# A projection stage continued inside the feed-forward block before it, and transposes of the first projection alternated with its first products

## The chip, the cores and the metric

The kernel runs on one core of one Trainium2 chip. The metric is device time in microseconds (us) of one execution; the time before the change is 2881.29 us, the median of 3 runs (2877.69 to 2884.19). TensorE is PE in the rows, VectorE is DVE, ScalarE is ACT, GpSimd is POOL, and SP is SyncE's queue.

## The reference

Two transformer blocks run one after the other on x of 1024 tokens by 1024 channels, all in float32:

```python
def first_block(x, ...):
    h = rms_norm(x, mix_norm_g) @ w_in            # 1024 x 2568: q, k, v, 8 forget gates, z
    merged = concat(rms_norm(forgetting_attention(q, k, v, log_f)), rms_norm(spatial_gating(gelu(z))))
    x = x + merged @ w_out
    gate, up = split(rms_norm(x, ffn_norm_g) @ w_gate_up)     # 1024 x 2*2816
    x = x + (silu(gate) * up) @ w_down
    return rms_norm(x, final_norm_g)

def second_block(x, ...):
    proj = rms_norm(x, w_norm_mix) @ w_mix_in     # 1024 x 3592: short conv, gated delta net, stick-breaking attention
    x = x + concat(y_sc, y_gdn, y_sb) @ w_mix_out
    gate, val = split(causal_dwconv(rms_norm(x, w_norm_ffn) @ w_ffn_up, w_ffn_conv))
    x = x + (silu(gate) * val) @ w_ffn_down
    return rms_norm(x, w_norm_final)
```

## The kernel before

Every product of float32 matrices is made of three TensorE products of rounded halves: value = hi + lo, and hi x hi, hi x lo, lo x hi are summed in PSUM. The activations stand transposed in SBUF as `xt_hi` and `xt_lo` (8 slices of 128 channels, 1024 tokens). Weights come in slices of 128 x 512: SyncE loads one into one of four `w_raw` buffers, GpSimd splits it into `w_hi` and `w_lo` (lines 115 and 117, or 278 and 280, 950 and 952), TensorE uses it. Semaphores order all this: `m.loaded`, `m.split`, `m.used`; PSUM has eight banks of 128 x 512.

The program is a list of stages, each a block of five instruction lists, one for each engine; a stage starts when all engines have left the one before. The ones that matter here:

- `first_stage` (projection 1). Tokens are normed in pairs of 128-token tiles: VectorE and ScalarE each square one tile (`square`, `square_pair`), ScalarE makes the reciprocal root, VectorE scales both tiles (`scale`). TensorE transposes half the tokens of one channel slice with four 128 x 128 transposes into a bank (`turn(h, k)`, half h, slice k, line 295); ScalarE rounds the bank to `xt_hi` (`high`), VectorE writes the rest to `xt_lo` (`low`, line 438). Four banks, 4 to 7, serve the transposes in rotation, so `turn` number n waits for `low` number n-4. TensorE does all eight `turn(0, k)` first, then the first chunk of products for the first half of the tokens (lines 315 to 317, banks 0 to 3), with the `turn(1, ...)` pairs after slices 3 to 6, then the second half.
- `mlp_stage` (output projection, norm, feed-forward). It is used twice, plain and with the causal convolution (tiles with `_conv`). The hidden channels go in 11 steps of 256: `up` products, hidden values, `down` products added to `x_sb`. The last step has its own code: its `up` slices 4 to 7 go to `end_hi` and `end_lo`, its four down slices go to the ring `w_hi`, `w_lo` again, and `split_slices(m, pool, last + 12, DN)` makes GpSimd wait until the down products of the step before are through with that ring place. TensorE waits for all four (`pe.wait_ge(m.split, last + 12 + DN)`), then does the last down products tile by tile (lines 1044 to 1046, `last_hi`, `last_lo`).
- The end of the plain `mlp_stage`: for each tile t VectorE adds the two banks (`last_down`, line 1375), ScalarE squares and makes the root (`square_rstd`, line 1120), VectorE scales by the gain (`normed`, line 1381), ScalarE squares again, VectorE scales into `scaled_out` (`rescale`, line 1387), SyncE stores `x_sb` to DRAM. Then TensorE transposes all of `scaled_out` in 16 turns over eight banks (line 1102), ScalarE writes `xt_hi` (line 1208), VectorE `xt_lo` (`low`, line 1234). GpSimd splits the first four slices of the next projection once all tiles are scaled.
- `proj2_stage` (projection 2). SyncE loads 8 gate columns (`w_ab`), GpSimd splits them, TensorE multiplies them with all tokens (lines 1482 to 1484, 48 products), then does seven chunks of 512 columns with `chunk_products` (line 169), 192 products each. ScalarE empties the banks and turns the gate values; VectorE scans them; TensorE transposes them (`gate_columns`, in chunk 1); then the convolution jobs follow the chunks.

Of the kernel before, what the change touches and what calls it, by code (L numbers as in the profile page):

```python
# [5 lines left out]
ALU = mybir.AluOpType  # L6
# [6 lines left out]
P = 128  # L13
# [171 lines left out]
def first_stage(m, x_sb, zu, zv, v, q, k_, sp_f, csum, sums_dram, w_sT):  # L185
# [34 lines left out]
    with nc.Block() as block:  # L220
# [67 lines left out]
        def _(pe):  # L288
# [130 lines left out]
        def _(dve):  # L419
# [30 lines left out]
            dve.tensor_copy(m.cols[:, COL_FFC + 88:COL_FFC + 132], m.psum[0][:, 2 * P:2 * P + 44]).then_inc(cols_done, 1)  # L450
            dve.wait_ge(cols_done, 3)
# [10 lines left out]

            dve.wait_ge(vec_turned, 2)
# [389 lines left out]
def mlp_stage(m, tag, w_out, scales, load_x, gcol, w_up, w_down, x_sb, conv, gain, store, next_gcol=None, first=None):  # L853
# [17 lines left out]
    spare = [m.at(f"scaled_out{i}" + tag, [P, 4, D], (16, 152)[i]) for i in range(2)]  # L871
    junk = m.at("mlp_squares" + tag, [P, 4, D], 176)
# [12 lines left out]
    GU, DN = 8, 4  # L885

# [8 lines left out]
    with nc.Block() as block:  # L895
        @block.sync
        def _(sp):
# [26 lines left out]
            if first is not None:  # L924
                load_first(m, sp, base + 16 + 12 * FI, first)
# [3 lines left out]
            sp.wait_ge(stored, 16 * NT)  # L929

        @block.gpsimd
        def _(pool):
# [25 lines left out]
            split_slices(m, pool, last + 12, DN)  # L958
            if first is not None:
                pool.wait_ge(scl, 2 * NT)  # L960
                split_first(m, pool, base + 16 + 12 * FI)

        @block.tensor
        def _(pe):
# [76 lines left out]
            def down_bank(hi, lo, bank, t, nh, done):  # L1041
                for j in range(2):
                    u, tok = 2 * nh + j, slice(t * P, (t + 1) * P)
                    pe.matmul(m.psum[bank][:, :], hi[:, j, tok], m.w_hi[:, u, :], start=j == 0, stop=False)  # L1044
                    pe.matmul(m.psum[bank][:, :], lo[:, j, tok], m.w_hi[:, u, :], start=False, stop=False)  # L1045
                    mm = pe.matmul(m.psum[bank][:, :], hi[:, j, tok], m.w_lo[:, u, :], start=False, stop=j == 1)  # L1046
# [39 lines left out]
            for t in range(NT):  # L1086
                if t in (0, 4):
                    pe.wait_ge(hid, 4 * (FI - 1) + 2 * (t // 4) + 2)
                for nh in range(2):
                    if t >= 4:  # L1090
                        pe.wait_ge(dn_ev, 16 * (FI - 1) + NB + 2 * (t - 4) + nh + 1)
                    down_bank(last_hi, last_lo, (2 * t + nh) % NB, t, nh, dn_done)
            if next_gcol is not None:
                for n in range(2 * KD):
                    h, k = n // KD, n % KD
                    if k == 0:
                        pe.wait_ge(scl, NT + 4 * (h + 1))
                        pe.wait_ge(dn_ev, 16 * FI + NB)
                    if n >= NB:
                        pe.wait_ge(t_lo, 16 + n + 1 - NB)  # L1100
                    for j in range(4):
                        mm = pe.transpose(m.psum[n % NB][:, j * P:(j + 1) * P], spare[h][:, j, k * P:(k + 1) * P], m.ident[:, :])
                    mm.then_inc(turned, 1)
# [12 lines left out]
        counts = {"square": 0, "log": 0, "rstd": 0}  # L1116

# [12 lines left out]
        def _(act):  # L1130
# [66 lines left out]
            for t in range(NT + 1):  # L1197
                if t < NT:
                    act.wait_ge(dn_ev, 16 * (FI - 1) + NB + 2 * t + 2)
                    square_rstd(act, 1, t, junk[:, t % 2, :])  # L1200
# [1253 lines left out]
```

## Time and profile before

| what | us |
|---|---|
| median of 3 runs | 2881.29 |
| the profiled execution, its own time | 2874.96 |
| span of the profiled execution | 2872.9 |
| TensorE busy in the span | 2724.7 (95%) |
| VectorE busy | 1298.7 (45%) |
| GpSimd busy | 1175.0 (41%) |
| ScalarE busy | 665.7 (23%) |

The times of the rows below are those of the profiled execution, from the start of its span. A row of the timeline gives start, duration, engine, line, operation, output and input, count, and in brackets the idle time of the engine just before and what ended it.

### The profile page before, as it was taken

Reading aid. Unit: us, or ns where it says so; the run is one execution under the profiler, and the core shown is the slowest. Engines: PE = TensorE matmul, PEld = TensorE weight load, DVE = VectorE, ACT = ScalarE, POOL = GpSimd, SP = SyncE. Lnnn points to the kernel's source line nnn. Section 1 sums busy time; section 2 is a strip of 40 time slices with the busy share of each in tenths; the row PEclk is TensorE's granted clock in tenths of the full one; section 3 lists DMA queues with packets and bytes.
Section 4 is the critical chain, followed back from the end, with each engine's and each line's share of the span. In section 5 each row is a group of like instructions: output and inputs, shape, how many; then the busy total and the mean of one; then the engine's idle time right before and its main releaser. Section 6 shows DMA issues by size and latency. Waiting matters only on the chain. (4 is left out here: it accounts for less than half of the span.)

```text
span 2872.9 us, 34847 instructions
## 1 busy us (share of the span) xinstructions
PE 2724.7 (95%) x12979; PEld 2183.2 (76%) x12979; DVE 1298.7 (45%) x1808; ACT 665.7 (23%) x1250; POOL 1175.0 (41%) x919
## 2 busy tenths in 40 slices
PE   7999879999999999979999888879999999999998
PEld 6786447888888888857888677864688888888876
DVE  3133432334333333461451466667234555666667
ACT  2201651200000001141222233245222211111123
POOL 4441134244444444423454333340324454555552
PEclk9999999999999999989999899989999999999999
DMA  3111003111111111121111000000311111111111
GB/s 121 47 48 37 30 16 117 30 52 47 51 47 49 49 48 47 55 89 39 50 48 41 1 1 1 1 16 1 118 30 41 48 44 51 47 50 48 47 55 73
DMA packets 91017, 131.61 MB, mean 46 GB/s; under 512 B 9269, under 2 KB 57632, under 8 KB 90920
## 3 DMA queue, kind: packets, MB, share of 16 engines
q1 hardware_dynamic: 88288, 121.76, 14.0%
q10 hardware_dynamic: 2632, 8.51, 0.7%
q8 instruction: 67, 1.10, 0.2%
q14 instruction: 30, 0.25, 0.0%
HBM read 121.82 MB, written 8.42 MB: 45 GB/s over the span
## 5 line engine op out<-in xcount | busy, mean ns | idle before, releaser
L115 POOL TENSOR_TENSOR w_hi<-w_raw,zero 128x512 fp32r<-128x512 f32 x336 | 395.1, 1176 | 1063.6 <-PE bank L1012 450.5
L117 POOL TENSOR_TENSOR w_lo<-w_raw,w_hi 128x512 fp32r<-128x512 f32 x336 | 485.0, 1443 | 26.4
L1010 PE MATMUL bank<-xt_hi,w_hi 128*128 128x512 f32 x1248 | 485.7, 389 | 1.6 <-DVE x_sb L1220 0.8
L1011 PE MATMUL bank<-xt_lo,w_hi 128*128 128x512 f32 x1248 | 485.5, 389 | 0.0
L1012 PE MATMUL bank<-xt_hi,w_lo 128*128 128x512 f32 x1248 | 485.5, 389 | 0.0
L1318 DVE TENSOR_TENSOR x_sb<-bank,x_sb 128x512 f32<-128x512 f32 x320 | 221.3, 692 | 202.9 <-PE bank L1046 202.5
L1010 PEld LDWEIGHTS bank<-xt_hi,w_hi 128*128 128x128 f32 x1248 | 234.2, 188 | 51.1 <-DVE x_sb L1220 1.3
L1012 PEld LDWEIGHTS bank<-xt_hi,w_lo 128*128 128x128 f32 x1248 | 234.2, 188 | 48.7
L1011 PEld LDWEIGHTS bank<-xt_lo,w_hi 128*128 128x128 f32 x1248 | 234.2, 188 | 48.6
L169 PE MATMUL bank<-xt_hi,w_hi 128*128 128x512 f32 x512 | 199.4, 390 | 0.0
L169 PE MATMUL bank<-xt_lo,w_hi 128*128 128x512 f32 x512 | 199.2, 389 | 0.0
L169 PE MATMUL bank<-xt_hi,w_lo 128*128 128x512 f32 x512 | 199.2, 389 | 0.0
L1276 DVE COPY hidden_raw<-bank 128x512 f32<-128x512 f32 x44 | 30.5, 692 | 326.0 <-PE bank L1012 325.9
L1285 DVE SCALAR_TENSOR_TENSOR hidden_conv<-hidden_raw_conv,cols,hidden_conv 128x1024 f32<-128x1024 f32 x80 | 156.0, 1979 | 6.6 <-ACT hidden_conv L1143 1.3
L1764 POOL TENSOR_TENSOR LM<-LT,levels 128x1024 f32<-128x1024 f32 x24 | 64.1, 2677 | 155.1 <-DVE LT L1912 83.8
L1044 PE MATMUL bank<-w_hi,hidden_hi 128*128 128x512 f32 x320 | 124.5, 389 | 0.0
L1045 PE MATMUL bank<-w_hi,hidden_lo 128*128 128x512 f32 x320 | 124.5, 389 | 0.0
L1044 PE MATMUL bank<-w_hi,hidden_hi_conv 128*128 128x512 f32 x320 | 124.5, 389 | 0.0
L1045 PE MATMUL bank<-w_hi,hidden_lo_conv 128*128 128x512 f32 x320 | 124.5, 389 | 0.0
L1046 PE MATMUL bank<-w_lo,hidden_hi 128*128 128x512 f32 x320 | 124.5, 389 | 0.0
L1046 PE MATMUL bank<-w_lo,hidden_hi_conv 128*128 128x512 f32 x320 | 124.5, 389 | 0.0
L169 PEld LDWEIGHTS bank<-xt_hi,w_hi 128*128 128x128 f32 x512 | 96.1, 188 | 20.4 <-ACT ab L1523 0.4
(466 smaller groups left out, 4820.0 us busy)
## 6 DMA issues: line engine op xcount, KB each, us to landing
w_raw<-in_w_gate_up_dram SPq DMA_DIRECT2D x88, 256.0 KB, 3.1
w_raw<-in_w_ffn_up_dram SPq DMA_DIRECT2D x88, 256.0 KB, 3.1
w_raw<-in_w_mix_in_dram SPq DMA_DIRECT2D x56, 256.0 KB, 2.7
w_raw<-in_w_down_dram SPq DMA_DIRECT2D x44, 256.0 KB, 2.8
w_raw<-in_w_ffn_down_dram SPq DMA_DIRECT2D x44, 256.0 KB, 2.8
w_raw<-in_w_in_dram SPq DMA_DIRECT2D x40, 256.0 KB, 2.7
x_sb<-in_x_dram SPq DMA_DIRECT2D x4, 1024.0 KB, 8.4
gate_rows<-gate_sums SPq DMA_DIRECT2D x8, 512.0 KB, 4.6
```

Source lines behind the costliest of these rows:

```text
L115: pool.tensor_tensor(m.w_hi[:, u, :], m.w_raw[:, u, :], zeros, ALU.add).then_inc(m.hi_done, 1)
L117: pool.tensor_tensor(m.w_lo[:, u, :], m.w_raw[:, u, :], m.w_hi[:, u, :].bitcast(F32), ALU.subtract).then_inc(m.split, 1)
L169: mm = pe.matmul(m.psum[b][:, :], lhs, rhs, start=k == 0 and i == 0, stop=k == KD - 1 and i == 2)
L1010: pe.matmul(m.psum[b][:, :], u_hi[:, col], m.xt_hi[:, k, tok], start=k == 0, stop=False)
L1011: pe.matmul(m.psum[b][:, :], u_hi[:, col], m.xt_lo[:, k, tok], start=False, stop=False)
L1012: mm = pe.matmul(m.psum[b][:, :], u_lo[:, col], m.xt_hi[:, k, tok], start=False, stop=k == KD - 1)
L1044: pe.matmul(m.psum[bank][:, :], hi[:, j, tok], m.w_hi[:, u, :], start=j == 0, stop=False)
L1045: pe.matmul(m.psum[bank][:, :], lo[:, j, tok], m.w_hi[:, u, :], start=False, stop=False)
L1046: mm = pe.matmul(m.psum[bank][:, :], hi[:, j, tok], m.w_lo[:, u, :], start=False, stop=j == 1)
L1285: ins = dve.scalar_tensor_tensor(mix[:, c, :], raw[:, c, PAD - back:PAD - back + S], weights_of(i, c, 2 - back), mix[:, c, :], ALU.mult, A ...
L1318: dve.tensor_tensor(xs, m.psum[t][:, :], xs, ALU.add).then_inc(dn_ev, 1)
L1764: pool.tensor_tensor(LM[j % 2][:, :, :], LT[:, :, :], lev[:, j, :].unsqueeze(1).to_broadcast([P, NT, P]), ALU.mult).then_inc(pool_s, 1)
```

## The change

There are four parts.

1. `proj2_stage` no longer opens a block. It returns an object whose five functions are called at the end of the plain `mlp_stage`'s five lists. No engine waits there for the others.
2. The join itself. The 16 turns of `scaled_out` use banks 0 to 3 in rotation. The rounding of turns 0 and 1 is queued on ScalarE and VectorE at tile 6 of the last tile loop, that of turns 2 and 3 at tile 7, the rest behind it (`turns_at`). The first chunk of projection 2 goes by token halves: TensorE turns slices 0 to 7 of the first half, multiplies the first half into banks 4 to 7 with the turns of the second half in pairs after slices 3 to 6, then the second half into banks 3 to 0. The gate columns' products follow chunk 0 instead of preceding it, and `gate_columns` moves from chunk 1 to chunk 2. Slices 4 to 7 of chunk 0 are split into `end_hi`, `end_lo`. ScalarE waits for the stores of `x_sb` before it empties chunk 0. Two scratch tiles move.
3. In `mlp_stage`, both uses: the four down slices of the last step are split into `end_hi`, `end_lo`, as soon as the last `up` products no longer read these.
4. In `first_stage`: `turn(0, 4)` to `turn(0, 7)` go one ahead of each of the products of slices 0 to 3; the pairs of `turn(1, ...)` follow slices 4 to 7 instead of 3 to 6; the waits of the first half for `t_lo` 5 to 8 go. On VectorE the copies of the gain columns come before `scale(1)`, and the copy of the identity to bfloat16 goes behind the last `low`.

```diff
@@ first_stage, TensorE
-            for k in range(KD):
+            for k in range(4):
                 turn(0, k)
             pe.wait_ge(cols_done, 3)
             for h in range(2):
                 for k in range(KD):
+                    if h == 0 and k < 4:
+                        turn(0, 4 + k)
...
                     for b in range(4 * h, 4 * h + 4):
-                        if k == 0:
-                            pe.wait_ge(t_lo, 5 + b if h == 0 else 9 + b)
+                        if h and k == 0:
+                            pe.wait_ge(t_lo, 9 + b)
...
-                    if h == 0 and 3 <= k < 7:
-                        turn(1, 2 * (k - 3))
-                        turn(1, 2 * (k - 3) + 1)
+                    if h == 0 and k >= 4:
+                        turn(1, 2 * (k - 4))
+                        turn(1, 2 * (k - 4) + 1)
@@ first_stage, VectorE
-            for j in range(2):
-                square(j)
-                scale(j)
-            dve.wait_ge(masked, 1)
-            dve.tensor_copy(m.ident_b[:, :], m.ident[:, :])
+            square(0)
+            scale(0)
+            square(1)
             dve.wait_ge(made, 5)
             dve.wait_ge(vec_turned, 1)
...
+            scale(1)
             dve.wait_ge(cols_done, 3)
...
+            dve.wait_ge(masked, 1)
+            dve.tensor_copy(m.ident_b[:, :], m.ident[:, :])
@@ mlp_stage, GpSimd
-            split_slices(m, pool, last + 12, DN)
-            if first is not None:
-                pool.wait_ge(scl, 2 * NT)
-                split_first(m, pool, base + 16 + 12 * FI)
+            for u in range(DN):
+                n = last + 12 + u
+                pool.wait_ge(m.used, last + RING + u + 1)
+                pool.wait_ge(m.loaded[u], 16 * (n // RING) + 16)
+                pool.tensor_tensor(end_hi[:, u, :], m.w_raw[:, u, :], zeros, ALU.add).then_inc(m.hi_done, 1)
...
+            if nxt is not None:
+                nxt.gpsimd(pool)
@@ mlp_stage, TensorE
+            def turn_next(h, k):
+                n = KD * h + k
+                pe.wait_ge(scl, NT + 4 * (h + 1))
+                if n < 4:
+                    pe.wait_ge(dn_ev, 16 * (FI - 1) + NB + 8 + n + 1)
+                else:
+                    pe.wait_ge(t_lo, 16 + n - 3)
+                for j in range(4):
+                    mm = pe.transpose(m.psum[n % 4][:, j * P:(j + 1) * P], spare[h][:, j, k * P:(k + 1) * P], m.ident[:, :])
+                mm.then_inc(turned, 1)
+
+            if nxt is not None:
+                for k in range(KD):
+                    turn_next(0, k)
+                nxt.tensor(pe, turn_next, t_lo, dn_ev)
@@ mlp_stage, ScalarE and VectorE
+        turns_at = {NT - 2: (0, 1), NT - 1: (2, 3), NT: tuple(range(4, 2 * KD))}
...
+            if nxt is not None:
+                act.wait_ge(stored, 16 * NT)
+                nxt.scalar(act)
@@ proj2_stage, GpSimd
+        for u in range(RING):
+            n = base + u
+            pool.wait_ge(m.used, n + 1 - 2 * RING)
+            split_slice(m, pool, n, n // RING, u, True)
+        for u in range(RING):
+            n = base + RING + u
+            pool.wait_ge(m.used, n + 1 - 2 * RING)
...
@@ proj2_stage, TensorE
+        for h in range(2):
+            for k in range(KD):
...
+                pe.wait_ge(m.split, base + k + 1)
+                pe.wait_ge(t_lo, 16 + 8 * h + k + 1)
+                for n in range(4):
+                    bank, col = m.psum[4 + n - 4 * h], slice(n * P, (n + 1) * P)
+                    if k == 0 and h == 0:
+                        pe.wait_ge(dn_ev, nxt.dn + 4 + n + 1)
+                    if k == 0 and h:
+                        pe.wait_ge(t_lo, 16 + 13 + n)
...
+                if h == 0 and 3 <= k < 7:
+                    turn(1, 2 * (k - 3))
+                    turn(1, 2 * (k - 3) + 1)
```

## Rows read from the trace of the kernel before

**Rows 1.** The page, part 1: busy time, share of the span, instructions.
```profile
PE 2724.7 (95%) x12979; PEld 2183.2 (76%) x12979; DVE 1298.7 (45%) x1808; ACT 665.7 (23%) x1250; POOL 1175.0 (41%) x919
```

**Rows 2.** Waits of PE: engine, line, releaser: total us, times, longest.
```profile
PE bank L1044 <- POOL w_lo L117: 8.3, 2, 4.2
```

**Rows 3.** Timeline of the first projection's start, several engines.
```profile
15.38 6.12 PE L295 MATMUL bank<-ident,x_scaled 128*128 128x128 f32 x32 [3.52 <-DVE x_scaled L432]
...
17.81 2.76 DVE L438 SCALAR_TENSOR_TENSOR xt_lo<-bank,cols,xt_hi 128x512 fp32r<-128x512 f32 x4 [0.83 <-ACT xt_hi L377]
...
19.07 1.06 PE L295 MATMUL bank<-ident,x_scaled 128*128 128x128 f32 x4
...
26.17 0.77 PE L315 MATMUL bank<-w_hi,xt_hi 128*128 128x512 f32 x1 [4.67 <-DVE xt_lo L438]
...
27.92 1.79 DVE L427 CUSTOM_DVE_ANT_0 junk_d<-x_sb 128x1024 f32<-128x1024 f32 x1
...
30.36 2.48 DVE L432 TENSOR_SCALAR x_scaled<-x_sb,x_rstd 128x1024 f32<-128x1024 f32 x2 [0.65 <-ACT x_rstd L372]
...
32.37 1.62 POOL L280 TENSOR_TENSOR first_lo<-w_raw,first_hi 128x512 fp32r<-128x512 f32 x1
...
39.24 1.03 PE L295 MATMUL bank<-ident,x_scaled 128*128 128x128 f32 x8
...
53.75 0.39 PE L315 MATMUL bank<-w_hi,xt_hi 128*128 128x512 f32 x1
```

**Rows 4.** Windows: stretch, us, busy by engine (instructions), PEclk, DMA, GB/s.
```profile
26.00:30.50 4.50, 4.33 (x10) 3.47 (x11) 3.85 (x7) 0.71 (x4) 4.34 (x4) 0.50 0.00 0
...
1267.00:1268.00 1.00, 1.00 (x6) 1.00 (x6) 0.44 (x1) 0.97 (x3) 0.00 (x0) 0.50 0.99 406
...
1269.00:1270.00 1.00, 1.00 (x8) 0.97 (x6) 0.75 (x1) 1.00 (x3) 0.00 (x0) 0.68 0.32 131
...
1298.60:1342.40 43.80, 43.80 (x193) 35.96 (x192) 10.85 (x9) 9.05 (x13) 18.18 (x14) 1.00 0.16 43
```

**Rows 5.** Timeline, plain feed-forward's end and projection 2's start, several engines.
```profile
1234.33 0.69 DVE L1318 TENSOR_TENSOR x_sb<-bank,x_sb 128x512 f32<-128x512 f32 x1 [0.67 <-PE bank L1046]
...
1237.15 1.26 POOL L117 TENSOR_TENSOR w_lo<-w_raw,w_hi 128x512 fp32r<-128x512 f32 x1
...
1238.47 0.50 PE L1044 MATMUL bank<-w_hi,last_hi 128*128 128x512 f32 x1 [4.17 <-POOL w_lo L117]
...
1242.45 0.39 PE L1045 MATMUL bank<-w_hi,last_lo 128*128 128x512 f32 x1
...
1264.23 1.04 ACT L1120 ACTIVATE mlp_squares<-x_sb 128x1024 f32<-128x1024 f32 x1
...
1264.85 5.35 PE L1102 MATMUL bank<-ident,scaled_out 128*128 128x128 f32 x32 [2.72 <-DVE x_sb L1375]
...
1270.63 9.34 ACT L1208 ACTIVATE xt_hi<-bank,cols 128x512 fp32r<-128x512 f32 x16
...
1271.43 10.62 DVE L1234 SCALAR_TENSOR_TENSOR xt_lo<-bank,cols,xt_hi 128x512 fp32r<-128x512 f32 x16
...
1285.32 0.59 PE L1482 MATMUL bank<-xt_hi,w_ab_hi 128*8 128x512 f32 x1 [7.49 <-POOL w_ab_lo L1473]
...
1342.43 0.39 PE L169 MATMUL bank<-xt_hi,w_hi 128*128 128x512 f32 x1
```

**Rows 6.** Timeline, the last step of the feed-forward with convolution.
```profile
2796.70 11.64 DVE L1336 SCALAR_TENSOR_TENSOR hidden_conv<-hidden_raw_conv,cols,hidden_conv 128x512 f32<-128x512 f32 x8 [0.85 <-ACT hidden_conv L1161]
...
2817.92 0.74 DVE L1336 SCALAR_TENSOR_TENSOR hidden_conv<-hidden_raw_conv,cols,hidden_conv 128x512 f32<-128x512 f32 x1
...
2837.71 0.69 DVE L1318 TENSOR_TENSOR x_sb<-bank,x_sb 128x512 f32<-128x512 f32 x1 [0.67 <-PE bank L1046]
...
2841.84 0.79 PE L1044 MATMUL bank<-w_hi,last_hi_conv 128*128 128x512 f32 x1 [4.17 <-POOL w_lo L117]
...
2846.66 0.39 PE L1046 MATMUL bank<-w_lo,last_hi_conv 128*128 128x512 f32 x1
```

More of the change, by code:

```diff
@@ L1395, in _ @@
                     rescale(t - 2)
+                for n in turns_at.get(t, ()) if nxt is not None and t < NT - 1 else ():
+                    low(16 + n, n % 4, next_gcol)
             normed(NT - 1)
[L1397 removed]
+            if nxt is not None:
                 rescale(NT - 2)
+                for n in turns_at[NT - 1]:
+                    low(16 + n, n % 4, next_gcol)
                 rescale(NT - 1)
[L1400 to L1403 removed]
+                for n in turns_at[NT]:
+                    low(16 + n, n % 4, next_gcol)
+                nxt.vector(dve)
     m.slices += 16 + 12 * FI
     m.chunks += FI
+    if nxt is not None:
+        m.slices += nxt.slices
+        m.chunks += nxt.chunks
 HG = 4
 def proj2_stage(m, sc, qkv, gz, sqk, sv, gates):
[L1415 to L1416 removed]
+    a, nxt = m.a, Machine()
     w = a["w_mix_in_2"][0]
[L1418 to L1419 removed]
+    wf = m.at("w_ab", [P, KD, 8], 196.125)
+    wf_hi, wf_lo = m.at("w_ab_hi", [P, KD, 8], 196.375, F32R), m.at("w_ab_lo", [P, KD, 8], 196.625, F32R)
     conv = m.at("conv", [P, 2, S], 184)
@@ new lines, in tensor, with gate_columns, wait_bank @@
+    def tensor(pe, turn, t_lo, dn_ev):
+        base, c0 = nxt.base, nxt.c0
+        for h in range(2):
+            tok = slice(h * HALF, (h + 1) * HALF)
+            for k in range(KD):
+                if k < RING:
+                    hi, lo = m.w_hi[:, k, :], m.w_lo[:, k, :]
+                else:
+                    hi, lo = nxt.hi[:, k - RING, :], nxt.lo[:, k - RING, :]
+                pe.wait_ge(m.split, base + k + 1)
[6 more added lines that the diff above has]
+                        pe.wait_ge(t_lo, 16 + 13 + n)
+                    pe.matmul(bank[:, :], hi[:, col], m.xt_hi[:, k, tok], start=k == 0, stop=False)
+                    pe.matmul(bank[:, :], hi[:, col], m.xt_lo[:, k, tok], start=False, stop=False)
+                    mm = pe.matmul(bank[:, :], lo[:, col], m.xt_hi[:, k, tok], start=False, stop=k == KD - 1)
+                    if h and n == 3:
+                        mm.then_inc(m.used, 1)
+                    elif k == KD - 1:
+                        mm.then_inc(m.bank_done, 1)
+                if h == 0 and 3 <= k < 7:
+                    turn(1, 2 * (k - 3))
+                    turn(1, 2 * (k - 3) + 1)
+        pe.wait_ge(f_split, 2)
+        for h in range(2):
+            tok = slice(h * HALF, (h + 1) * HALF)
+            pe.wait_ge(evac, h + 1)
+            for k in range(KD):
+                pe.matmul(m.psum[4 + h][0:8, :], wf_hi[:, k, :], m.xt_hi[:, k, tok], start=k == 0, stop=False)
+                pe.matmul(m.psum[4 + h][0:8, :], wf_hi[:, k, :], m.xt_lo[:, k, tok], start=False, stop=False)
+                mm = pe.matmul(m.psum[4 + h][0:8, :], wf_lo[:, k, :], m.xt_hi[:, k, tok], start=False, stop=k == KD - 1)
+            mm.then_inc(f_done, 1)
+        def gate_columns():
+            pe.wait_ge(rows, 3)
+            pe.wait_ge(evac, 2 * NB)
+            for j in range(NT):
+                pe.transpose(m.psum[NB - 1][:, 8 * j:8 * j + 8], gc[:, j * P:(j + 1) * P], m.ident[0:8, 0:8])
+            for j in range(NT):
+                mm = pe.transpose(m.psum[NB - 1][:, 64 + 8 * j:72 + 8 * j], ab[:, j * P:(j + 1) * P], m.ident[0:8, 0:8])
+            mm.then_inc(turned, 1)
+        for c in range(1, NC):
+            def wait_bank(b):
+                if c == 1 and b in (4, 5):
+                    pe.wait_ge(f_evac, b - 3)
+                elif c == 1:
+                    pe.wait_ge(evac, (b + 4) % NB + 1)
+                else:
+                    pe.wait_ge(evac, 8 * (c - 1) + b + 1)
+                if c == 2 and b == 3:
+                    gate_columns()
+                if c == 2 and b == NB - 1:
+                    pe.wait_ge(turned, 2)
+            chunk_products(m, pe, base + 8 * c, c0 + c, c == 5, wait_bank)
```

361 lines of the change are left out of this document (169 added, 192 removed).

## The prediction

> **What bounds the kernel.** I read the page's busy shares first: TensorE is busy 95% of the span, no other engine half of it [rows 1]. So what can be won without fewer products is TensorE's idle time and the time it spends at a lower clock. The view of TensorE's waits names the places. One entry is touched by part 3 of the change: twice TensorE waits some 4 us for GpSimd's last split [rows 2]. The timelines around the edits then show each idle stretch with its releaser: 4.67 us at 26 us [rows 3]; 4.17, 2.72 and 7.49 us around 1238 to 1285 us (and a further 2.12 between the two halves of the transposes there) [rows 5]; 4.17 us again at 2842 us [rows 6]. These come to 25 us, 0.9% of the span. Last the windows: each longer stop is followed by a spell in which the granted clock is 0.50, the 1.2 GHz level: 10 products in 4.33 us at 26 us [rows 4], 0.43 us each, against 43.80 us for 193 at 2.4 GHz, 0.227 each [rows 4]. A product in such a spell costs 0.20 us more.
>
> **Part 4, the first projection.** Before, TensorE does 32 transposes from 15.38 on, then stands until 26.17, because the products' start asks for the `low` of slices 4 to 7, which stand in VectorE's list behind `square(2)` and `scale(2)`; its second half starts at 53.75 [rows 3]. After, `turn(0,4)` starts at 19.07 as before (the sixteenth transpose's end sets it, and the first `low` is done at 18.5) [rows 3]. At the clock of then, the turn ends near 19.8. From there to the second half stand 96 products (21.8 us), `turn(0,5)` to `(0,7)` and eight turns of the second half. A turn costs 0.456: between products, eight transposes push TensorE back by 0.91 (the row at 39.24 shows them [rows 3]; four pairs and their products fill 39.24 to 53.75 in this measure). That is 19.8 + 21.8 + 11 x 0.456 = 46.6. The weights don't hold it: the last split is through at 33.99 [rows 3], and it is wanted near 43.
>
> One new wait. `turn(0,7)` now ends near 29.4, so `low(0,7)` ends near 31.1, and `square(3)` and `scale(3)` stand behind it in VectorE's list. Before, `square(3)` started at 27.92 and `scale(3)` ended at 32.84, 4.9 later [rows 3]. Counted from 31.1 this is 36.0; GpSimd's last weight split ends at 33.99, after which I take the scaling somewhat faster, 35.6. `turn(1,0)` is wanted at 34.9: a stall of 0.7 (bounds 0 and 1.5). The second half starts at 47.3 instead of 53.75: **6.4 us** (5 to 7). The column copies moved ahead of `scale(1)` fit in the time in which VectorE waits for ScalarE's root. The identity copy costs nothing where it goes: VectorE is idle for the second half's products, and its reader is in the next stage.
>
> The trace also bears on whether transposes hold the clock up. In the stretch from 1264.85 TensorE does transposes alone; the clock is 0.50 at 1267 and has risen within 1269 to 1270 (0.68 over that us) [rows 4, 5]. So transposes alone let it rise, and I let the products at 19.8 start at 2.4 GHz, with no spell such as that of 26 to 30.5. The Trainium skill says the opposite in "TensorE: Matmul & The Clock Gate", section "Part 4: PE-mode transpose": transposes don't count as busy time for the clock. By it the products would begin at the lower level and the sum be as in rival A below.
>
> **Part 3, the last down slices.** TensorE starts the last down products at 1238.47, released by GpSimd. What is needed besides is VectorE's read of the bank at 1234.33 + 0.69 = 1235.02 [rows 5]. GpSimd can now split in the time in which it was idle since the last `up` products; so TensorE starts at 1235.1, 3.4 us earlier. The stop shrinks to 0.8 us and I take it to be without a spell at half clock (if not, the 3.4 alone stay); there were 3.98 us from 1238.47 to 1242.45 for 10 products worth 2.27, 1.7 more [rows 5]. The chain behind moves by **5.1 us**. In the convolution's copy the reads end at 2837.71 + 0.69 = 2838.4, the products start at 2841.84 [rows 6]: 3.4; the first 11 take 4.82 instead of 2.50: 2.3; together 5.7. Everything behind this to the end of the span is paced by these products, so it counts in full. Against it: GpSimd's four splits now fall on VectorE's tap steps. Such a step takes 0.74 alone, and 11.64/8 = 1.46 where GpSimd works beside it [rows 6]; four to five steps would lag by 3 us, and the last reads, without steps between, win most of it back. I charge 0.5 (0 to 2). **5.2 us** (3.4 to 5.7).
>
> **Parts 1 and 2, the join.** What sets its pace is ScalarE's chain of 16 square-and-root groups, 1.60 us each (four of them from 1264.23 to 1270.63) [rows 5]. The fifteenth ends at 1269.03. It comes 5.1 earlier by part 3: 1263.9. Into the chain come the `xt_hi` of turns 0 and 1, 9.34/16 = 0.58 each: 1.2. Then the square of tile 7 waits for VectorE's list, which has the two `low` (10.62/16 = 0.66 each) ahead of the two reads of tile 7: 0.8 for the second `low` and 1.3 for the reads, 2.1. So the fifteenth group ends at 1267.2. Turns 2 and 3 are rounded behind it: 1.2 on ScalarE, then 0.8 for the last `low`: 1269.2. Only then is the bank of `turn(0,7)` free; the turn costs 0.9 at half clock. First product at **1270.1**. Queued behind the same `low`s are `rescale` of tiles 6 and 7, wanted only by the second half's turns at 1283; behind the new wait for the stores stands the emptying of chunk 0's banks, first needed by the gate products at 1320, when the stores are long out.
>
> Before, with all 16 turns done, TensorE began projection 2 at 1285.32 and chunk 1 at 1342.43 [rows 5]: 57.1 us for gate products and chunk 0, with a half-clock spell at its head. After, the same products start 15.2 earlier, again after a stop and so with the same spell, and the eight turns of the second half lie between them, 3.65. That is 11.6 earlier. Removed in this are the wait for all rounding, the block's end, and the trip for `w_ab`, whose load, split and products are now covered by chunk 0. Chunk 0's slices are split in time: slices 0 to 3 while the last down products run, 4 to 7 at about 1255 to 1266, first wanted at 1283. But then GpSimd works beside VectorE's scaling. What `L1336` shows doubles an instruction [rows 6]; up to three of them lie on the path, 0 to 3 us; most fall in the 3 us in which VectorE waits for turn 0's rounding, so 0.5. **11.1 us** (7 to 13). `gate_columns` in chunk 2 waits for nothing new, since the scan is done by 1350; ScalarE's first convolution job waits some 2 us longer, under a chunk of 43.8 us.
>
> **Sum.** 6.4 + 11.1 + 5.2 = 22.7 us. The profiled execution's own time is 2874.96 (span 2872.9 and 2.1 around it), which gives 2852.3; the median of the runs is 6.3 higher, 2881.29, and the prediction for it is **2858.6**. A difference of under 0.2%, 5.8 us, can't be told from none here.
>
> **Rivals.** A: transposes don't keep the clock up. Then the first projection's products start at half clock, ten of them at 0.20 more, 2.0 to 2.2 lost: 2860.8. Against it stands the rise within 1269 to 1270 [rows 4].
> B: VectorE's order sets the join. The `low`s put ahead of tile 7 and GpSimd's splits stretch the tile loop by 5 more than I count, and the 0.7 stall becomes 1.5: gain 17, 2864.5. For it: VectorE is nearly full in the tile loop, and doubled instructions are in the trace [rows 6].
> C: part 3 does not do what it says: the last down products wait for something else that comes at the same time (the hidden values, or a late load), so 5.1 and 5.2 go; gain 12.4, 2868.9. Against it: VectorE's reads before them end on TensorE's beat in both copies [rows 5, 6].
> D, on the other side: the lower clock persists in the join. TensorE comes in with 7.5 us of idle time cut up by single turns, and if it then ran chunk 0 at 1.2 GHz throughout, 192 products would cost 38.4 us instead of the 2.2 of one spell: 36.2 - 22.7 = 13.5 us slower, 2894.8. It decides from some 125 products at half clock. Against it: every spell in the rows ends within 5 us of work [rows 4 to 6].
>
> **Chances.** Forecast 0.74, A 0.10, B 0.09, C 0.05, D 0.02. The first three reach from 2852 (all upper bounds, 7 + 13 + 5.7 = 25.7, and half of the runs' scatter) to about 2865; with C at the edge the range is 2851 to 2869. Faster by over 0.2%: 0.96, same 0.02, slower 0.02.
>
> **What would show it.** The first product of the first projection near 20 with granted clock 1.00, its second half at 47 to 48, an idle time near 0.7 before `turn(1,0)`. The last down products following the reads by 0.1, with products of 0.39 only, in both copies. Projection 2's first product near 1264 in the new count (1270.1 less the 6.4 won before), chunk 1 starting 17.5 earlier than 1342.43, no wait for the gate columns. The prediction is wrong if TensorE shows a new wait above 2 us in one of these places, or if chunk 0 runs at 0.50 for more than 5 us.

## The result and the profile after

| | kernel before | kernel after |
|---|---|---|
| median, us (runs) | 2879.49 (4: 2875.12 to 2884.19) | 2849.26 (4: 2848.04 to 2851.25) |
| profiled execution's own time | 2874.96 | 2850.17 |
| its span | 2872.9 | 2848.3 |

The ratio is 0.9895, 95% interval 0.9877 to 0.9913: the change makes the kernel 1.0% faster, 30 us in these medians. The forecast was 2858.6 with a range from 2851 to 2869: the right side, but 9.3 us too slow and outside the range. Two more sets of runs of the same program gave 2852.22 (ratio 0.9909) and 2849.26 (0.9904). One of these three medians, 2852.22, would lie inside the range. All 12 runs of the changed kernel have the median 2850.35 and the mean 2850.4; 67 runs of the kernel before have 2878.0 and 2878.6. (One further execution of the kernel before, at 4605 us with the clock at 0.555, is left out everywhere.) So the gain in means is 28.2 us, and 22.7 were forecast.

The page's part 1 of the kernel after, as [rows 1] of before: TensorE has the same 12979 products and transposes in 11.8 us less busy time. So nearly half of what the span lost, 24.6 us, is not idle time but the same work done in less time; 1.7 us of the 11.8 lie in the three unedited stages shown below. Stretches that TensorE spends at 1.2 GHz instead of 2.4 are called half clock from here on.

```profile
PE 2712.9 (95%) x12979; PEld 2175.6 (76%) x12979; DVE 1300.9 (46%) x1808; ACT 669.8 (24%) x1252; POOL 1180.3 (41%) x919
```

TensorE's waits in the kernel after. The 8.3 us for GpSimd's last split [rows 2] are gone; in their place stand 1.7 us, twice 0.8, that no releaser explains. The join now waits twice for `low`, 9.4 us in all; before, its three stops were 2.72, 2.12 and 7.49 us:

```profile
PE bank L1115 <- DVE xt_lo L1255: 9.4, 2, 5.8
...
PE bank L1058 <- issue: 1.7, 2, 0.8
```

The timeline of the first projection after, against [rows 3]. Twenty transposes, then products at once; VectorE's `scale(3)`; the last pair of turns of the second half; the first product of the second half:

```profile
16.31 4.47 PE L295 MATMUL bank<-ident,x_scaled 128*128 128x128 f32 x20 [3.15 <-DVE x_scaled L434]
20.49 0.52 PE L317 MATMUL bank<-w_hi,xt_hi 128*128 128x512 f32 x1
20.85 0.39 PE L318 MATMUL bank<-w_lo,xt_hi 128*128 128x512 f32 x1
...
33.71 1.42 DVE L434 TENSOR_SCALAR x_scaled<-x_sb,x_rstd 128x1024 f32<-128x1024 f32 x2 [0.65 <-ACT x_rstd L374]
...
46.60 1.03 PE L295 MATMUL bank<-ident,x_scaled 128*128 128x128 f32 x8
47.39 0.48 PE L317 MATMUL bank<-w_hi,xt_hi 128*128 128x512 f32 x1
```

The second half starts at 47.39 instead of 53.75. No stop stands ahead of `turn(1,0)`, which starts at 35.69: `scale(3)` ends at 35.13.

The timeline at the plain block's end and the join, against [rows 5]. Two GpSimd splits and VectorE's two scalings of the last tile, with GpSimd idle, are among the rows:

```profile
1231.11 0.69 DVE L1339 TENSOR_TENSOR x_sb<-bank,x_sb 128x512 f32<-128x512 f32 x1 [0.67 <-PE bank L1060]
1231.90 0.47 PE L1058 MATMUL bank<-end_hi,last_hi 128*128 128x512 f32 x1 [0.83 <-issue]
1232.21 0.39 PE L1059 MATMUL bank<-end_hi,last_lo 128*128 128x512 f32 x1
...
1253.22 2.25 DVE L1402 SCALAR_TENSOR_TENSOR x_sb<-x_sb,mlp_rstd,gain 128x1024 f32<-128x1024 f32 x1
...
1254.35 2.02 POOL L1520 TENSOR_TENSOR end_hi<-w_raw,zero 128x512 fp32r<-128x512 f32 x1
...
1255.39 1.53 DVE L1408 TENSOR_SCALAR scaled_out<-x_sb,mlp_rstd 128x1024 f32<-128x1024 f32 x1
...
1259.24 1.74 PE L1115 MATMUL bank<-ident,scaled_out 128*128 128x128 f32 x8 [3.54 <-DVE xt_lo L1255]
...
1260.98 1.06 ACT L1139 ACTIVATE mlp_squares<-x_sb 128x1024 f32<-128x1024 f32 x1 [2.10 <-DVE x_sb L1396]
...
1261.47 2.13 POOL L1522 TENSOR_TENSOR end_lo<-w_raw,end_hi 128x512 fp32r<-128x512 f32 x1
...
1262.39 1.75 DVE L1408 TENSOR_SCALAR scaled_out<-x_sb,mlp_rstd 128x1024 f32<-128x1024 f32 x1
...
1264.07 1.27 DVE L1402 SCALAR_TENSOR_TENSOR x_sb<-x_sb,mlp_rstd,gain 128x1024 f32<-128x1024 f32 x1
...
1265.27 0.74 DVE L1408 TENSOR_SCALAR scaled_out<-x_sb,mlp_rstd 128x1024 f32<-128x1024 f32 x1
...
1266.81 1.94 PE L1115 MATMUL bank<-ident,scaled_out 128*128 128x128 f32 x8 [5.83 <-DVE xt_lo L1255]
...
1268.40 0.78 PE L1548 MATMUL bank<-xt_hi,w_hi 128*128 128x512 f32 x1
...
1270.10 0.40 PE L1549 MATMUL bank<-xt_lo,w_hi 128*128 128x512 f32 x1
...
1327.41 0.39 PE L169 MATMUL bank<-xt_hi,w_hi 128*128 128x512 f32 x1
```

The last row is chunk 1. From the start of the last down products to it are 95.5 us; before, from 1238.47 to 1342.43, 104.0 [rows 5]. The convolution's copy now runs as the plain one:

```profile
2818.67 0.69 DVE L1339 TENSOR_TENSOR x_sb<-bank,x_sb 128x512 f32<-128x512 f32 x1 [0.67 <-PE bank L1060]
...
2819.47 0.47 PE L1058 MATMUL bank<-end_hi_conv,last_hi_conv 128*128 128x512 f32 x1 [0.83 <-issue]
```

**Where the rest is.** The edited places are covered by four stretches between fixed products of TensorE; three stretches hold code that the diff doesn't touch: attention, the gated delta net, and the stick-breaking attention with the products up to the last block's first. The windows of these three, in the profile of before and of after (columns as in [rows 4]):

```profile
266.80:438.40 171.60, 137.23 (x922) 78.77 (x921) 79.70 (x254) 97.58 (x235) 43.37 (x38) 0.94 0.08 28
1606.20:1869.50 263.30, 223.31 (x1536) 196.80 (x1536) 164.58 (x273) 85.86 (x136) 91.87 (x64) 0.91 0.00 1
1902.00:2052.40 150.40, 133.00 (x512) 70.42 (x513) 99.21 (x208) 71.37 (x157) 39.22 (x33) 0.91 0.09 33
```

```profile
260.60:435.10 174.50, 140.18 (x921) 80.61 (x921) 79.70 (x254) 97.82 (x235) 43.40 (x38) 0.92 0.08 27
1591.20:1853.00 261.80, 221.52 (x1536) 196.16 (x1536) 164.59 (x273) 85.86 (x136) 92.82 (x63) 0.92 0.00 1
1885.50:2033.30 147.80, 130.12 (x512) 68.58 (x513) 99.21 (x208) 71.30 (x157) 36.81 (x30) 0.93 0.07 26
```

The same instructions take 171.6 us in one and 174.5 in the other, 263.3 and 261.8, 150.4 and 147.8; VectorE's busy time is the same to 0.1, TensorE's is not, and the granted clock goes the other way than the length. In this pair the sum differs by only 1.2 (585.3 and 584.1). Whether it is more on average is what the later experiments ask.

### The profile page after: what moved, and what is told of

Same layout as the page of the kernel before. It is cut to its first block and busy times, and to the rows that moved or that the text cites. A ratio compares the mean times of both kernels' runs of the same rounds, so it can differ in the third digit from the quotient of the medians.

```text
span 2848.3 us, 34838 instructions
## 1 busy us (share of the span) xinstructions
PE 2712.9 (95%) x12979; PEld 2175.6 (76%) x12979; DVE 1300.9 (46%) x1808; ACT 669.8 (24%) x1252; POOL 1180.3 (41%) x919
## 5 line engine op out<-in xcount | busy, mean ns | idle before, releaser
L115 POOL TENSOR_TENSOR w_hi<-w_raw,zero 128x512 fp32r<-128x512 f32 x324 | 384.0, 1185 | 1006.7 <-PE bank L1026 450.2
L1024 PE MATMUL bank<-xt_hi,w_hi 128*128 128x512 f32 x1248 | 485.7, 389 | 1.6 <-DVE x_sb L1241 0.8
L1026 PE MATMUL bank<-xt_hi,w_lo 128*128 128x512 f32 x1248 | 485.5, 389 | 0.0
L1025 PE MATMUL bank<-xt_lo,w_hi 128*128 128x512 f32 x1248 | 485.5, 389 | 0.0
L117 POOL TENSOR_TENSOR w_lo<-w_raw,w_hi 128x512 fp32r<-128x512 f32 x324 | 468.4, 1446 | 25.3
L1024 PEld LDWEIGHTS bank<-xt_hi,w_hi 128*128 128x128 f32 x1248 | 234.2, 188 | 51.0 <-DVE x_sb L1241 1.3
L169 PE MATMUL bank<-xt_hi,w_hi 128*128 128x512 f32 x448 | 174.4, 389 | 0.0
L169 PE MATMUL bank<-xt_lo,w_hi 128*128 128x512 f32 x448 | 174.3, 389 | 0.0
L169 PE MATMUL bank<-xt_hi,w_lo 128*128 128x512 f32 x448 | 174.3, 389 | 0.0
L1154 ACT ACTIVATE hidden_raw<-bank 128x512 f32<-128x512 f32 x44 | 26.3, 601 | 360.9 <-PE bank L1026 360.8
```

Of the source, the lines that this page charges most:

```text
L115: pool.tensor_tensor(m.w_hi[:, u, :], m.w_raw[:, u, :], zeros, ALU.add).then_inc(m.hi_done, 1)
L117: pool.tensor_tensor(m.w_lo[:, u, :], m.w_raw[:, u, :], m.w_hi[:, u, :].bitcast(F32), ALU.subtract).then_inc(m.split, 1)
L169: mm = pe.matmul(m.psum[b][:, :], lhs, rhs, start=k == 0 and i == 0, stop=k == KD - 1 and i == 2)
L1024: pe.matmul(m.psum[b][:, :], u_hi[:, col], m.xt_hi[:, k, tok], start=k == 0, stop=False)
L1025: pe.matmul(m.psum[b][:, :], u_hi[:, col], m.xt_lo[:, k, tok], start=False, stop=False)
L1026: mm = pe.matmul(m.psum[b][:, :], u_lo[:, col], m.xt_hi[:, k, tok], start=False, stop=k == KD - 1)
```

## The experiments

**The theories.** They are named as in the expectations. S: each part gives its term at its own place, as the prediction says, and what the medians show beyond the sum is how the half-clock time of unedited stages happens to fall in an execution. P: the shifted start of those stages changes their half-clock time for good. B (rival B of the prediction): VectorE's order and GpSimd's splits set the join, so its part is small.

**Each part alone.** Three kernels. The first is the kernel before with part 4:

```diff
-            for k in range(KD):
+            for k in range(4):
                 turn(0, k)
...
+                    if h == 0 and k < 4:
+                        turn(0, 4 + k)
```

> The kernel before with part 4 alone (the first projection's order). Theory S (the gain is the sum of the four places where TensorE stopped, 6.2 + 11.8 + 5.5 = 23.5 us by the two profiled executions, and what the medians show beyond it, some 6.7 us, is how the half-clock spells of other stages happen to fall in one execution): 6.2 us faster than before, second half of the first projection at 47.5, and the attention stage's length free to vary by some 3 us either way. Theory P (the shifted phase of the first projection itself changes the spells of the stages behind it for good): 10 us or more faster, or under 3, the same in all rounds.

Measured: 2869.52 us median of 12, ratio 0.9968 (0.9958 to 0.9979), which is neither the 10 us or more nor the under 3 that P asked for.

The second is the kernel before with part 3 in both blocks (and the scratch tiles placed as in the kernel after):

```diff
-            split_slices(m, pool, last + 12, DN)
+            for u in range(DN):
+                n = last + 12 + u
+                pool.wait_ge(m.used, last + RING + u + 1)
...
-                    down_bank(last_hi, last_lo, (2 * t + nh) % NB, t, nh, dn_done)
+                    down_bank(last_hi, last_lo, (2 * t + nh) % NB, t, nh, dn_done, end_hi, end_lo)
```

> The kernel before with part 3 alone, in both feed-forward blocks (the four last down slices split early; the scratch and scaled_out tiles placed as in the changed kernel). Theory S: 5.1 us in the plain block, all of it kept, since the chain behind moves with the last down products, and 5.5 in the block with convolution: 10.6 us faster. Rival (the plain block's part is lost at the join because the next stage's first slices are split late): 5.5 us.

Measured: 2862.72 us median of 6, ratio 0.9950 (0.9935 to 0.9964). Its last down products start as in the kernel after:

```profile
1236.25 0.47 PE L1051 MATMUL bank<-end_hi,last_hi 128*128 128x512 f32 x1 [0.83 <-issue]
```

The third is the kernel after with parts 3 and 4 undone, so that the join alone is left:

> The changed kernel with parts 3 and 4 undone: the join alone (parts 1 and 2). Theory S: 11.8 less the 5.1 of part 3, 6.7 us faster than before; GpSimd splits the first slices later but still ahead of their use. Rival (the parts need each other: without the early split the four slices of projection 2 come late and TensorE waits for GpSimd): under 3 us.

Measured: 2869.97 us median of 12, ratio 0.9974 (0.9964 to 0.9983). The timeline of its join:

```profile
1242.46 0.50 PE L1048 MATMUL bank<-w_hi,last_hi 128*128 128x512 f32 x1 [4.17 <-POOL w_lo L117]
...
1271.48 1.94 PE L1105 MATMUL bank<-ident,scaled_out 128*128 128x128 f32 x8 [3.56 <-DVE xt_lo L1245]
1280.83 1.94 PE L1105 MATMUL bank<-ident,scaled_out 128*128 128x128 f32 x8 [7.41 <-DVE xt_lo L1245]
```

What follows: by their profiles, outside the three untouched stages, these kernels are 7.0, 11.3 and 5.6 us shorter than the kernel before. That adds to 23.9; the whole change has 24.4. The parts act nearly separately, the first half of S holds, and the two rivals in the expectations (5.5 us for part 3, under 3 for the join) fell. The join is the exception: from the last down products to the delta net it alone is 5.0 us shorter, where beside part 3 it brings 6.0; without part 3 its second wait is 7.4 us instead of 5.8 (why was not tried). In means of whole runs, against the 2878.6 of before, the three gain 8.3, 15.4 and 8.4 us. That is 1.3, 4.1 and 2.8 more than outside the three stages; the first of these is no more than the scatter. The gains add to 32.1, where the whole change has 28.2. So what is gained beyond the edited places doesn't show as one term of one part.

**The changed kernel again**, to see what one program's scatter is:

> The changed kernel once more, profiled and timed beside the next two. Theory S (the four places give 23.5 us by the profiles; the rest of the 28 to 30 us between the medians is half-clock time in untouched stages, which differs from execution to execution): again 27 to 30 us under the kernel before, while the lengths of the attention, delta and read stages differ from the first profile of the same kernel by up to 3, 8 and 3 us. Rival (each kernel has its own fixed spells): those three lengths are the same as in the first profile within 0.3 us.

Measured: 2852.22 us, median of 4, ratio 0.9909 (0.9893 to 0.9924). That is 26 us under the kernel before, a little less than the 27 to 30 expected. Its profile has attention 171.8 us instead of 174.5 and the last of the three stages 150.4 instead of 147.8, with nearly the same sum, 583.8. So single stages change from execution to execution, and the rival, the same lengths within 0.3 us, fell; the rest was 2266.7 and 2266.1 us.

**The join without its second stop.** The turns 4 to 7 of the first half go one ahead of each of the first four product groups, as in part 4:

```diff
-                for k in range(KD):
+                for k in range(4):
                     turn_next(0, k)
...
+                if h == 0 and k < 4:
+                    turn(0, 4 + k)
```

> The changed kernel with turns 4 to 7 of the first half one ahead of each of the first four product groups at the join, as part 4 does in the first projection. If turn 7's wait for the rounding queued behind tile 7 (5.8 us of TensorE's idle time) is what sets the first product, the products of slices 0 and 1 start 5 to 6 us earlier and the kernel is 4 to 5.5 us faster than the changed one, some 28 by profile and 35 by median against before. If VectorE's tile loop sets it whatever the order (the first products then delay turns 6 and 7, and the second half's turns follow late), under 1 us.

Measured: 2850.21 us median of 5, ratio 0.9907 (0.9892 to 0.9923), no different from the kernel after, where 4 to 5.5 us were expected. Yet the join is 6.4 us shorter, 352.9 against 359.3 us from the last down products to the delta net, and TensorE's waits have one entry for it instead of two:

```profile
PE bank L1115 <- DVE xt_lo L1255: 3.6, 1, 3.6
```

The delta net's stage behind it took all of it back: 268.0 us instead of 261.8. I ran it a second time:

> The alternating join a second time. If its first profile is typical (join 6.4 us shorter than the changed kernel's, the stage after it 268.0 us long instead of 261.7), it comes again to about 2850 us, with that stage near 268. If that stage's length in the first profile was chance, it comes to 2844 to 2846 us, with that stage near 262.

Measured: 2851.08 us median of 6, ratio 0.9902 (0.9885 to 0.9918), one run of the six at 2836.82, the others from 2848.07 to 2854.17. The profiled one is that at 2836.82, which neither of the two expected outcomes has. The windows of the delta net in the two profiles of this one program, whole and its first 20 us:

```profile
1581.70:1849.70 268.00, 227.80 (x1537) 201.19 (x1537) 164.54 (x273) 85.83 (x136) 91.90 (x64) 0.89 0.00 1
1581.70:1601.70 20.00, 19.99 (x73) 13.54 (x74) 9.84 (x25) 7.19 (x14) 8.52 (x27) 0.66 0.01 2
```

```profile
1581.80:1839.70 257.90, 217.60 (x1536) 192.50 (x1536) 164.37 (x273) 85.81 (x136) 91.87 (x63) 0.93 0.00 1
1581.80:1601.80 20.00, 17.73 (x80) 11.27 (x80) 11.44 (x28) 9.88 (x16) 8.86 (x28) 0.83 0.01 2
```

The same instructions, started at the same time within 0.1 us, take 10.1 us more in one execution; TensorE is busy 10.2 us longer, no other engine is. At the stage's head the granted clock is 0.66 against 0.83. So the second half of S holds for single executions: this stage's time depends on how much of it TensorE spends at 1.2 GHz, and its start time doesn't fix that.

**Added work that moves the start.** The first 12 gate products of projection 2 are done twice (2.8 us at full clock), or the first 24 (5.6 us); the repeated ones are overwritten by the real ones:

```diff
+            for k in range(4 if h == 0 else 0):
+                pe.matmul(m.psum[4 + h][0:8, :], wf_hi[:, k, :], m.xt_hi[:, k, tok], start=k == 0, stop=False)
+                pe.matmul(m.psum[4 + h][0:8, :], wf_hi[:, k, :], m.xt_lo[:, k, tok], start=False, stop=False)
+                pe.matmul(m.psum[4 + h][0:8, :], wf_lo[:, k, :], m.xt_hi[:, k, tok], start=False, stop=k == 3)
```

In the changed kernel, 12 and 24 more:

> The changed kernel with 12 more products of the gate columns between chunk 0 and chunk 1 (repeated, their result is overwritten by the same): 2.8 us more work for TensorE on its path, everything behind it 2.8 us later. If untouched stages have fixed lengths: 2.8 us slower than the changed kernel. If their half-clock time depends on when they begin: anything from 4 us faster to 9 us slower, and the delta stage's length moves with it.

> As the one before with 24 more products, 5.6 us. Fixed lengths: 5.6 us slower than the changed kernel and 2.8 slower than with 12. Dependence on the start: not in this proportion.

Measured: 2850.71 us (4 runs, 2849.32 to 2851.09) with 12, so nothing for 2.8 us of work, and 2863.30 us (6 runs, 2851.61 to 2866.16) with 24, some 13 for 5.6. So the stages behind don't have fixed lengths. The profiles' delta stage has 258.5 and 266.4 us. The alternating join with 12 more:

> The alternating join and 2.8 us of repeated gate products. If the half-clock time of the stage after the join depends on when that stage begins, its length leaves 268.0 us and the total lies below that of the alternating version without added work, down to 2844 us. If the stages have fixed lengths, the total is 2.8 us above it, 2853 us.

Measured: 2846.64 us median of 6 (2842.07 to 2857.13), ratio 0.9888 (0.9869 to 0.9907): 3 to 4 us less than without the added work, but in six runs that span 15, so not clear of the scatter. It is what the expectation had for lengths that aren't fixed.

**Profiles of the kernel before.** Three more:

> The kernel before, profiled again. Theory S: the untouched stages' lengths differ from the first profile (attention 171.6, delta 263.3, from stick-breaking to the second feed-forward 150.4) by some us, and the own time lies near the median 2878 rather than at the first profile's 2875. Rival: the same lengths within 0.3 us.

> A third profile of the kernel before. The two so far have 263.3 and 263.9 us between the end of the second projection's stage and the next read. Theory that untouched stages' length varies with the granted clock: an execution of above 2878 us has that stage or the attention some us longer, and the four touched places the same within 0.7 us.

> A fourth profile of the kernel before, for the same question: whether the executions differ in the lengths of untouched stages (attention 171.6 to 172.0 us, the stage before the stick-breaking read 263.3 to 263.9, the one after it 147.7 to 150.4 so far), while the four touched places stay the same within 0.7 us.

Measured: 2874.36, 2879.73 and 2884.03 us; the first isn't near the 2878 expected, the other two have the longer stage that was expected of them. The one of 2884.03, same three windows as above:

```profile
268.50:440.30 171.80, 137.58 (x921) 78.70 (x920) 79.63 (x255) 97.36 (x235) 43.37 (x38) 0.94 0.08 27
1608.40:1878.70 270.30, 230.61 (x1536) 202.85 (x1536) 164.55 (x273) 85.79 (x136) 91.73 (x63) 0.87 0.00 1
1911.20:2061.60 150.40, 132.85 (x513) 70.39 (x514) 99.15 (x208) 71.32 (x157) 39.22 (x33) 0.91 0.09 33
```

Take the three stages from the own time of each of the four executions:

```
own time, us    the three stages            their sum   all the rest
2874.36         172.0 + 263.9 + 147.7       583.6       2290.8
2874.96         171.6 + 263.3 + 150.4       585.3       2289.7
2879.73         175.5 + 263.5 + 150.4       589.4       2290.3
2884.03         171.8 + 270.3 + 150.4       592.5       2291.5
```

The times differ by 9.7 us, the three stages by 8.9 and the rest by 1.8. That is more than the 0.7 expected; it is what the forget gates' first product moved, from 75.5 to 77.3 us. So the scatter of this kernel's runs is for the most part that of these three stages.

**Is the average length of the three stages the same in every kernel?** "Chance" says that each execution draws it anew from one spread; "place" says that it hangs on when the stages begin. Four more kernels, the last two being the kernel before with the same repeated gate products:

> The changed kernel a third time. Its profiles have 583.8 and 584.1 us in attention, delta and stick-breaking stage together and 2266.4 in all the rest; its eight times have a mean of 2850.8, so these three stages take 584.4 us on average, against 587.8 in the kernel before (2878.4 - 2290.6). Theory chance: the three stages' length is drawn anew in each execution from the same spread in every kernel; then the mean of more runs moves towards 2266.4 + 586 = 2852.5. Theory place: the length hangs on when the stages begin; then the mean stays at 2850.8 within 0.7.

> The changed kernel with 12 repeated gate products a second time. The rest of it takes 2269.6 us. Theory chance: the mean of its times is near 2269.6 + 586 = 2855.5. Theory place: it stays near 2850.5, where its first four times lay (2849.3 to 2851.1), with 581 us in the three stages.

> The kernel before with 12 of its gate products repeated, 2.8 us of TensorE work at full clock and nothing else; the delta and the stick-breaking stage begin 2.8 us later. Theory chance: mean 2.8 above that of the kernel before, within 1.5. Theory place: the sum of the three stages in its profiles leaves 587.8 us by several us, so that the mean is not 2.8 above.

> The kernel before with 24 of its gate products repeated, 5.6 us of TensorE work; the delta and the stick-breaking stage begin 5.6 us later. Theory chance: mean 5.6 above that of the kernel before, within 1.5. Theory place: the three stages together change by several us, so that the mean differs from that.

Measured: the changed kernel 2849.26 us median of 4 (mean 2849.7, where chance said 2852.5 and place 2850.8); with 12 more 2853.83 of 5 (mean 2852.0, chance 2855.5, place 2850.5); before with 12 more 2877.72 of 11 (ratio 1.0001, 0.9992 to 1.0010; mean 2878.6, where chance said 2881.4); before with 24 more 2884.85 of 9 (ratio 1.0024, 1.0014 to 1.0034; mean 2885.2, chance 2884.2). All runs of each program together; "rest" is the mean over its profiles, the last column the mean time less the rest:

```
kernel                     runs  mean     rest     three stages
before                      67   2878.6   2290.6   588.0
before + 12 products        11   2878.6   2293.3   585.3
before + 24 products         9   2885.2   2296.0   589.2
part 4 alone                12   2870.3   2283.6   586.7
part 3 alone                 6   2863.2   2279.3   583.9
join alone                  12   2870.2   2285.0   585.2
after                       12   2850.4   2266.2   584.2
after + 12 products          9   2851.3   2269.4   581.9
after + 24 products          6   2861.9   2271.1   590.8
alternating join            11   2849.9   2259.7   590.2
alternating join + 12        6   2847.2   2262.2   585.0
```

The kernel before, run beside the others each time, had means from 2878.2 to 2879.1 us in the four sets, so the sets don't make the differences. The rest follows the added work (2.7 and 5.4 for 2.8 and 5.6 in the kernel before). The three stages don't keep one mean: with runs that scatter by 2 to 5 us, a mean of 9 to 12 runs is good to 0.5 to 1.4, a rest that one profile gives is good to about 1, and 581.9 and 588.0 are much further apart than that. Chance alone fails: it was 2.8 and 3.5 us off in the two kernels with 12 products more, though only 1.0 in the kernel before with 24. The profiles show one of these differences in a single stage: the delta net took 261.6 to 261.9 us in all three of the changed kernel, and 258.5 and 258.7 in the two with 12 products more, 3.2 less, which is the 2.8 us of added work. So place holds in so far as 2.8 or 5.6 us of work ahead change the mean length in some kernels. That the later start does it, and not the added products themselves, is not shown, nor which start gives which length.

## Why the prediction was right and where it was wrong

**First projection, 6.4 forecast.** The profile pair gives 6.4 at the second half's first product, 47.39 where 47.3 was forecast. That the two agree so well is luck: the transposes began 0.9 later than in the profile that the working stood on (16.31 instead of 15.38), and the 0.7 stall that I had added did not come. Eight profiles without part 4 have the forget gates' first product at 75.5 to 77.3, mean 76.6; ten with it at 69.0 to 70.1, mean 69.5: 7.1 us. The profile of the working was the earliest of the eight. The mechanism is as told: 20 transposes and the first product at 20.49. The stall before `turn(1,0)` did not come: `scale(3)` took 1.42 us for two instructions, not 2.48 [rows 3]. GpSimd's last split had ended at 33.60, just before it; in [rows 3] one ran beside it.

**Part 3, 5.1 and 5.2 forecast.** With part 3 alone the two places are 5.7 and 5.5 us shorter. The products follow the read's end by 0.1 and are at 0.39 from the second on, after a stop of 0.83 us. The 0.5 for tap steps stretched by GpSimd's splits was not lost; in the kernel after, the three tap steps beside the splits took 0.77, 0.86 and 1.18 us instead of 0.74, and the last reads were on TensorE's beat.

**The join, with part 3's share 11.1 forecast.** 3.3 us come ahead of the last down products and 8.4 behind them, 11.7. The inner steps are off in both directions. From the last down products to the first product of projection 2 I had 35.0 us; it was 36.5. So that product stands at 1268.40 and not near 1264; the other 2.9 us are attention, which was that much longer in this execution. Chunk 1 is 15.0 us earlier, mostly for the same reason, not 17.5. ScalarE's wait for tile 7's square came as forecast, 2.1. What was under-priced is GpSimd beside VectorE: the scale by the gain took 2.25 and 1.60 us instead of 1.28, `rescale` 1.53 and 1.75 instead of 0.75, where I had charged 0.5 for all. In each of these four cases a GpSimd split ran beside it; with GpSimd idle the same two instructions took 1.27 and 0.74. The other way, four products ran at half clock at the head, 12 before: 1.5 us of the 2.2 by which the way from projection 2's first product to chunk 1, 59.0 us, was shorter than my 61.2 (the 0.5 counted in it). TensorE's two stops here, 3.54 and 5.83 us, are 9.4 where 7.5 were expected; read by its letter, the sign of being wrong (a new wait above 2 us) is met by them.

**Rivals.** A, transposes don't keep the clock up, did not come as priced: behind the 20 transposes the first product took 0.52 us and the second 0.39. But of the ten profiles with part 4 three still had a short spell there, three products at 0.63 or more and part of a fourth, some 0.7 us; the second profile of the changed kernel is one:

```profile
16.35 4.53 PE L295 MATMUL bank<-ident,x_scaled 128*128 128x128 f32 x20 [3.48 <-DVE x_scaled L434]
20.53 0.78 PE L317 MATMUL bank<-w_hi,xt_hi 128*128 128x512 f32 x1
21.11 0.63 PE L318 MATMUL bank<-w_lo,xt_hi 128*128 128x512 f32 x1
...
22.26 0.40 PE L318 MATMUL bank<-w_lo,xt_hi 128*128 128x512 f32 x1
```

The distance between transposes shows the level too: 0.21 us where the granted clock is 0.50, 0.11 where it is 1.00 (the stretch from 1264.85 [rows 4, 5], up to 1269.5 and from 1269.7 on). At the program's start they are 0.21 apart, although the profile's clock reads 1.00 there, so the 1.00 that the prediction names as a sign tells nothing. In three of the ten profiles, the third of the changed kernel among them, the distance fell to 0.11 while TensorE had done nothing but transposes, before the first product. The Trainium skill's "TensorE: Matmul & The Clock Gate", section "Part 4: PE-mode transpose", says that they don't count; here the traces decide against it. B fell as a whole: the join brought 6.0 us beside part 3's 5.7, and 5.0 alone, where the forecast had 6.0. Its mechanism, GpSimd's splits beside VectorE, was there, but cost 1.5 us and not 5. C fell with part 3 alone. D fell: chunk 0 was at full clock from 1270.1 on, 3.3 us after the transposes' start.

**The step that failed** is the sum's last: 22.7 us taken from the whole, as though everything else kept its length and the median stood where three runs put it. Of the 9.3 us, 3.3 are the base: 2881.29 was the median of three runs, over 67 runs it is 2878.0, and the profiled execution with 2874.96 wasn't 6.3 below it but 3.0. 1.6 are the edited places, 24.3 for 22.7. 3.8 are the three untouched stages, 588.0 us on average before and 584.2 after. What is left, 0.6, is within the scatter. The range's edge at 2851, which all 12 runs' median misses by 0.65 us, came from bounds on the edited places and half the runs' scatter; it had no term for a length in unedited code, which the three runs' own spread of 6.5 us could have told of, had I asked which stage it comes from.

**Open.** Why the three stages' half-clock time is what it is in a given execution and in a given kernel. No run varied something inside them. So the 3.8 us are measured, but not explained.

## What to carry to other kernels

A stop of TensorE of some 4 us costs its length and the half-clock products behind it; filling it with transposes or products already at hand wins both, and separate places nearly add up (7.0, 11.3 and 5.6 us against 24.4 together). Before you trust a gain smaller than the spread of the runs (here some 10 us, 0.35%), take the profile of several executions of the kernel before and find the stages whose length differs: their spread belongs in the range, and a local gain as clear as the alternating join's 6.4 us can fail to show in the median. Compare a change by the stretch it edits and by the whole, and don't explain the one by the other.

## What the runs showed of the hardware

- The same instructions from the same start time took 257.9 and 268.0 us, with mean granted clock 0.93 and 0.89; in all 18 profiles the delta net's stage took 257.9 to 270.4 us, attention 170.4 to 175.6, the last of the three stages 147.7 to 147.8 or 150.3 to 150.6 and nothing between.
- Adding 2.8 us of products to the kernel before left its time the same (ratio 1.0001, 0.9992 to 1.0010).
- A stop of 0.83 us left the products behind it at 0.39 us from the second on; one of 4.17 us was followed by ten at half clock [rows 5]. After stops of 3.5 and 5.8 us around two turns, the half clock ended 3.3 us after transposes had begun again, four products into the chunk.
- Transposes alone let the clock rise: their distance fell from 0.21 us to 0.11 before any product in three of ten profiles of the first projection.
- GpSimd's splits beside VectorE's scaling stretched VectorE's instructions of 1.28 us to 1.60 and 2.25, and those of 0.75 us to 1.53 and 1.75.
